# One streaming-encoder layer on one core: the program unrolled in groups of two tiles, without DRAM scratch, with a ring of seven slots and three buffers for the streamed weights

## The chip, the core and the metric

The kernel runs on one core of one Trainium2 chip. Its engines are TensorE (PE in the profile), VectorE (DVE), ScalarE (ACT), GpSimd (POOL) and SyncE (SP), each with its own instruction stream; they meet at semaphores. The metric is the device time of one execution in microseconds, as the median of several runs. All data is fp32.

## The reference

One layer over 1024 prompt frames and 32 sample frames of width 1024. Cut to what matters:

```
proj = rmsnorm(x) @ w_in                         # columns q|k|v|g (4 x 512), B|C|h (3 x 512)
q, k = rotary(q) * 128**-0.5, rotary(k)          # 4 heads of 128
o    = retention(state, q, k, v)                 # decayed scores @ v + decayed q @ state; state update
o    = rms_scale(o) * silu(g)
c    = B * short_conv(C * h)                     # 3 taps, 2 past rows
x    = x + concat[o, c] @ w_out
xn   = rmsnorm(x)
# PEER, per token and for each of 8 heads:
s1, s2 = keys1 . q1, keys2 . q2                  # 128 scores each
v1,i1 = top16(s1); v2,i2 = top16(s2)
top,sel = top16(v1[:,None] + v2[None,:])         # of 256 pairs
e    = i1[sel]*128 + i2[sel]; gate = softmax(top)
x    = x + sum_k gate_k * gelu(xn . u_tab[e_k]) * v_tab[e_k]      # 8 x 16 experts
y    = rmsnorm(x)
```

The state and the last two conv rows of both request groups are outputs too.

## The kernel before, in words

The tokens are nine tiles: eight of 128 prompt tokens and one of 32 sample tokens. For every token 128 expert rows (u and v side by side, 8 KB) are gathered from the table `uv`. One gather is an indirect DMA from GpSimd (line 445): one row for each of the 128 tokens of a tile, 1 MB, into one of `RING` = 8 slots of `ring`. Eight tiles of 128 gathers and one of 32 (the sample's tokens are spread over the partitions four times) make 1056.

What happens with gather k of a tile, in `experts` on each engine: VectorE multiplies the u half with `xn_cur` and sums it into `dots` (line 1033); ScalarE applies gelu (L585); VectorE multiplies with the gate (`weigh`, L1027), but only after the dot of gather k+1; ScalarE scales the v half (L581); TensorE adds it with eight transposing matmuls to `expert_sum` (L741) and raises `slot_free`, on which GpSimd waits before it gathers into the slot again.

Before all this, `projection` runs for all tokens, in two groups: GROUP_A (tile 0) and GROUP_C (the other seven prompt tiles and the sample). Its results go to DRAM, `proj_scratch` and `conv_scratch`. Between the gathers of tile t, the `mixer` of tile t+1 is woven in: a generator yields slot numbers (S_ROPE to S_PICK), `advance` runs its next piece when the loop has come to that slot, and each engine has the same slots, 64 per tile, one for two gathers. The mixer loads q, k, v, g from the scratch, does rotary, retention, W_out (L687), the second norm, the queries (L724; eight of the 16 weight blocks are resident, eight are streamed through two buffers `wq_buf`), the keys (L711), the top-16 search (L942 to L970) and the choice of indices and gates (L975 to L1006). The choice works on all eight heads of a tile at once, so that the index tile `idx_next` is complete only at its end; GpSimd copies it to `idx_cur` (L452) and then starts the next tile. The tiles 0 to 6 are a hardware loop (`Fori`) on each engine. At a tile's end ScalarE moves the sums out of PSUM (L596), TensorE transposes them back (L755) and the final norm writes y.

Each engine works in the order of its own program; a wait holds all that stands behind it. SP issues the loads in the same way.

Of the kernel before, what the change touches and what calls it, by code (L numbers as in the profile page):

```python
# [18 lines left out]
TILES = SEQ // P  # L35
H = 4
RET = H * P
CH = (D - RET) // P
PH = 8
# [5 lines left out]
SAMPLE_STEPS = STEPS // QUADS  # L45
RING = 8
PAIR = 2
SLOTS = STEPS // PAIR
WQ_RES = 8
WBUF = 2  # L50
STREAMED = BLK - WQ_RES
TOK_A = P
TOK_C = TOK - TOK_A
# [3 lines left out]
UNITS = CONV_UNITS + RET_UNITS  # L57
# [4 lines left out]
S_ROPE, S_KDECAY, S_QKT, S_SCORES, S_DECAYED, S_OUT, S_GATED, S_GATEDT = 2, 4, 5, 6, 7, 8, 9, 12  # L62
S_WOUT = 13
S_X1, S_XN, S_XNT = 21, 22, 23
S_QUERY = 25
S_TOP = 31
S_PAIRS = 47
S_BEST = 48
S_PICK = 56


class Group:
# [4 lines left out]

    def __init__(self, t0, tiles, buffers, earlier=None):
        self.t0, self.tiles, self.buffers = t0, tiles, buffers
        self.sample = tiles[-1] == DEC  # L80
        self.tok = sum(tiles)
        self.prompt = self.tok - (DEC if self.sample else 0)
        self.chunks = [(lo, min(lo + 512, self.tok)) for lo in range(0, self.tok, 512)]
        self.uses = [(3 * c + part, kind, i) for c in range(CH) for part, kind in enumerate("ChB")
                     for i in range(len(self.chunks))]
        self.conv_uses = len(self.uses)
        self.uses += [(CONV_UNITS + u, "tile", i) for u in range(RET_UNITS) for i in range(len(tiles))]
        self.by_act = [kind in ("tile", "C") for _, kind, _ in self.uses]

        self.block_ops = 5 + 4 * self.sample  # L90
        self.per = dict(uses=len(self.uses), act=sum(self.by_act), dve=len(self.uses) - sum(self.by_act),
                        ops=CH * self.block_ops, tiles=RET_UNITS * len(tiles), blocks=CH)
        self.before = {what: earlier.before[what] + earlier.per[what] if earlier else 0 for what in self.per}

        self.loads_before = [len(range(b, UNITS, earlier.buffers)) if earlier else 0 for b in range(buffers)]
        assert self.per["uses"] % 2 == 0 and self.conv_uses % 2 == 0

    def count(self, what, n=0):

        return self.before[what] + n  # L100

    def end(self, what):
        return self.count(what, self.per[what])

    def taken(self, q):

        who = "act" if self.by_act[q] else "dve"
        return who, sum(x == self.by_act[q] for x in self.by_act[:q + 1])

    def last_use(self, unit):  # L110
        return max(q for q, use in enumerate(self.uses) if use[0] == unit)

    def slot(self, q):

        return 1 + q * (SLOTS - 2) // len(self.uses)


GROUP_A = Group(0, [P], 4)
GROUP_C = Group(1, [P] * (TILES - 1) + [DEC], 2, GROUP_A)


def layer_kernel(nc, xT, x, w_ret, w_conv, w_out, wq, keysT, uv, g_mix, g_ffn, g_fin, conv_par,
                 ret_state, cos_sin, decay_p, decay_s, edge_p, edge_s, block_decay, ident, sel, iota,
                 y, out_ret_p, out_ret_s, out_conv_p, out_conv_s):
    proj = nc.dram_tensor("proj_scratch", (TOK, 4 * RET), F32).ap()
    convT = nc.dram_tensor("conv_scratch", (CH * P, TOK), F32).ap()

    with ExitStack() as ctx:
# [3 lines left out]
        def sem(name):  # L132
            return ctx.enter_context(nc.semaphore(name))


        ring = sb("ring", [P, RING, 2 * D])
        arena = sb("arena", [P, 7680])
# [3 lines left out]
        x1_next = sb("x1_next", [P, D])  # L141
        xn_next = sb("xn_next", [P, D])
        xn_cur = sb("xn_cur", [P, D])
# [3 lines left out]
        sel_sb = sb("sel_sb", [P, DEC])  # L147
# [6 lines left out]
        state = sb("state", [P, H, P])  # L154
        top_v = sb("top_v", [P, BLK, TOPK])
        top_i = sb("top_i", [P, BLK, TOPK], U32)
        idx_next = sb("idx_next", [P, STEPS], I32)
        idx_cur = sb("idx_cur", [P, STEPS], I32)
        gate_next = sb("gate_next", [P, PH, TOPK])
        gate_cur = sb("gate_cur", [P, STEPS])  # L160
        dots = sb("dots", [P, STEPS])
        weights = sb("weights", [P, STEPS])
        reduced = sb("reduced", [P, 2 * PH])
        stat = sb("stat", [P, 8])
# [3 lines left out]
        new_tail = sb("new_tail", [P, CH, 2, 2])  # L168


        flat = ring[:, :, :].rearrange("p r d -> p (r d)")
        xn_a = flat[:, 0:KC * TOK_A].rearrange("p (k t) -> p k t", k=KC)
        xn_c = flat[:, KC * TOK_A:KC * TOK].rearrange("p (k t) -> p k t", k=KC)
        at = KC * TOK
        units = [flat[:, at:at + KC * UNIT], flat[:, at + KC * UNIT:at + 2 * KC * UNIT],
                 arena[:, 0:KC * UNIT], arena[:, KC * UNIT:2 * KC * UNIT]]
        at += 2 * KC * UNIT
        rstd_all = flat[:, at:at + TOK]
        squares = flat[:, at + TOK:at + 3 * TOK].rearrange("p (b t) -> p b t", b=2)
        gate_c = flat[:, at:at + TOK_C]  # L180
        conv_y = flat[:, at + TOK_C:at + 2 * TOK_C + 2]
        conv_out = flat[:, at + 2 * TOK_C + 2:at + 3 * TOK_C + 2]
        taps = flat[:, at + 3 * TOK_C + 2:at + 4 * TOK_C + 6]
        assert at + 4 * TOK_C + 6 <= RING * 2 * D
        ones = xn_cur[:, 0:P]
        stored = xn_cur[:, P:P + 2 * UNIT].rearrange("p (b n) -> p b n", b=2)
        wq_buf = wq_sb[:, WQ_RES:]


        qkvg = arena[:, 0:2048]  # L190
        rot = arena[:, 2048:3072].rearrange("p (g c) -> p g c", g=2 * H)
        swap = arena[:, 3072:4096].rearrange("p (g c) -> p g c", g=2 * H)
        qkT = swap
        k_dec = arena[:, 4096:4608].rearrange("p (h c) -> p h c", h=H)
        decayed = arena[:, 4608:5120].rearrange("p (h c) -> p h c", h=H)
        ret_sq = decayed
        ret_o = arena[:, 5120:5632].rearrange("p (h c) -> p h c", h=H)
        catT = arena[:, 5632:6656].rearrange("p (k c) -> p k c", k=KC)
        xnT = catT
        qT = arena[:, 6656:7680].rearrange("p (g b c) -> p g b c", g=2, b=4)  # L200
        pairs = arena[:, 0:2048].rearrange("p (h i j) -> p h i j", h=PH, i=TOPK)
        scores = arena[:, 2048:4096].rearrange("p (b n) -> p b n", b=BLK)
        onehot = arena[:, 2048:4096].rearrange("p (k j) -> p k j", j=TOPK)
        left = arena[:, 5120:5376]
        best_v = arena[:, 5376:5504].rearrange("p (h k) -> p h k", h=PH)
        best_i = arena[:, 5504:5632].bitcast(U32).rearrange("p (h k) -> p h k", h=PH)
        half_i = arena[:, 5632:5888].bitcast(U32).rearrange("p (s k) -> p s k", s=2)
        half_f = arena[:, 5888:6144].rearrange("p (s k) -> p s k", s=2)
        pick_f = arena[:, 6144:6400].rearrange("p (s k) -> p s k", s=2)
        top_f = arena[:, 6400:6656].rearrange("p (b k) -> p b k", b=BLK)  # L210
        y_sb = arena[:, 6656:7680]
        sum_T = arena[:, 2048:3072].rearrange("p (k t) -> p k t", k=KC)
        folded_T = arena[:, 3072:3072 + KC * DEC].rearrange("p (k t) -> p k t", k=KC)


# [4 lines left out]
        bank = [expert_sum[:, 0:512], expert_sum[:, 512:D]]  # L220
        rms_ps = [x1_ps[:, 0:512], x1_ps[:, 512:D], tp[:, 1, 0:DEC]]


        consts_in = sem("consts_in")
        eps_set = sem("eps_set")
        xT_in = sem("xT_in")
        g_mix_in = sem("g_mix_in")
        unit_in = [sem(f"unit_in{i}") for i in range(GROUP_A.buffers)]
        squared = sem("squared")
        summed = sem("summed")  # L230
        rooted = sem("rooted")
        normed = sem("normed")
        projected = sem("projected")
        act_took = sem("act_took")
        dve_took = sem("dve_took")
        stored_out = [sem("stored_out0"), sem("stored_out1")]
        par_in = sem("par_in")
        conv_ops = sem("conv_ops")
        conv_out_done = sem("conv_out_done")
        tails_out = sem("tails_out")  # L240
        inits = sem("inits")

        tile_in = sem("tile_in")
        silu_done = sem("silu_done")
        rotated = sem("rotated")
        qkT_ready = sem("qkT_ready")
        qkT_copied = sem("qkT_copied")
        scores_ready = sem("scores_ready")
        decayed_ready = sem("decayed_ready")
        ret_ready = sem("ret_ready")  # L250
        ret_squared = sem("ret_squared")
        ret_rooted = sem("ret_rooted")
        gated = sem("gated")
        gatedT_ready = sem("gatedT_ready")
# [68 lines left out]
        def started(generator):  # L323
            return [generator, -1]
# [821 lines left out]
```

## Time and profile before

| | us |
|---|---|
| median of 3 runs (lowest, highest) | 3466.18 (3463.09, 3477.43) |
| the profiled execution | 3462.3 |
| its span, first to last instruction | 3459.0 |
| DVE busy | 2058.5 (60%) |
| PE busy | 2394.0 (69%), granted clock 0.824 on average |
| ACT busy | 1578.4 (46%) |
| DMA, mean over the span | 354 GB/s, 1225 MB |

The span is that of the profiled execution, the time is that of the whole execution around it. Busy shares are means over stages that differ much, so they are to be read by stage. A clock of 1.0 is 2.4 GHz for TensorE, 0.5 is 1.2 GHz, values between are means over a stretch.

### The profile page before, as it was taken

How to read it: one execution, taken by the hardware profiler on the slowest of the kernel's cores; microseconds unless marked ns; L12 is line 12 of the kernel's file. 1: busy time of each engine (PE TensorE's matmuls, PEld its weight loads, DVE VectorE, ACT ScalarE, POOL GpSimd, SP SyncE). 2: the span in 40 equal slices, each digit the busy share in tenths (PEclk: the TensorE clock that was granted, in tenths of full speed). 3: DMA queues.
4: the chain of work that ended last, by engine and by line, in shares of the span. 5: the costliest groups of instructions: out<-in, count | busy, mean ns of one | idle time of the engine just before them, and what ended most of it. 6: DMA issues, size and time to landing. Idle time of an engine off the chain costs nothing.

```text
span 3459.0 us, 43882 instructions
## 1 busy us (share of the span) xinstructions
PE 2394.0 (69%) x13716; PEld 1975.8 (57%) x13716; DVE 2058.5 (60%) x5356; ACT 1578.4 (46%) x2528; POOL 1256.1 (36%) x1076
## 2 busy tenths in 40 slices
PE   5799997676577657765776567647765676477756
PEld 4456885565457545754575457535754575346645
DVE  2121152568766876687668666866687667656774
ACT  1000113554555455445544554455545554455454
POOL 0000002444444544454344344434444444344434
PEclk8899997897789778976897799769977897778666
DMA  4612225999999999999999999989999999989987
GB/s 165 256 54 69 79 74 214 421 420 410 399 421 419 410 391 421 419 408 391 421 419 405 394 418 420 404 357 408 420 407 398 421 420 409 372 343 410 420 336 324
DMA packets 195395, 1225.07 MB, mean 354 GB/s; under 512 B 23568, under 2 KB 38864, under 8 KB 56592
## 3 DMA queue, kind: packets, MB, share of 16 engines
q0 software_dynamic: 152064, 1107.36, 78.0%
q1 hardware_dynamic: 32304, 103.66, 8.0%
q10 hardware_dynamic: 10752, 10.82, 0.9%
q8 instruction: 119, 1.95, 0.2%
q14 instruction: 156, 1.28, 0.1%
HBM read 1206.09 MB, written 15.67 MB: 353 GB/s over the span
## 4 chain that ended last, share of the span: by engine, by line
DMA 36%; PE 28%; issue 15%; DVE 13%; ACT 6%; SPq 1%; DVEq 0%; another core or an unknown queue 0%; POOL 0%; POOLq 0%; ACTq 0%; PEldq 0%
DMA ring<-in_uv,idx_cur 30%; PE expert_sum L741 8%; PE expert_sum L641 7%; PE expert_sum L647 5%; ACT ring L581 5%; PE mm L724 4%; DVE ring L1033 3%; DMA wq_sb<-in_wq 2%; DMA arena<-conv_scratch 2%; PE x_ps L687 1%; DVE arena L970 1%; DVE arena L988 1%; DVE arena L966 1%; DVE arena L968 1%; DVE arena L995 1%
## 5 line engine op out<-in xcount | busy, mean ns | idle before, releaser
L741 PE MATMUL expert_sum<-ident_sb,ring 128*128 128x128 f32 x8448 | 1421.6, 330 | 912.0 <-ACT ring L581 895.5
L741 PEld LDWEIGHTS expert_sum<-ident_sb,ring 128*128 128x128 f32 x8448 | 1207.9, 172 | 1139.0 <-ACT ring L581 1112.9
L445 POOL DMA_INDIRECT ring<-in_uv,idx_cur x1056 | 1245.1, 1179 | 1602.9 <-PE expert_sum L741 1339.7
L1033 DVE CUSTOM_DVE_ANT_0 ring<-ring,xn_cur 128x1024 f32<-128x1024 f32 x1056 | 1290.3, 1223 | 677.1 <-DMA ring<-in_uv,idx_cur 644.0
L581 ACT ACTIVATE ring<-ring,weights 128x1024 f32<-128x1024 f32 x1056 | 1196.3, 1134 | 0.0
L585 ACT ACTIVATE dots<-dots 128x1 f32<-128x1 f32 x1056 | 212.8, 201 | 1084.5 <-DVE dots L1033 1076.8
L724 PE MATMUL mm<-arena,wq_sb 128*128 128x128 f32 (+1 forms) x2304 | 311.6, 293 | 31.8 <-DMA wq_sb<-in_wq 31.8
L724 PEld LDWEIGHTS mm<-arena,wq_sb 128*128 128x128 f32 x2304 | 300.5, 210 | 36.8 <-DMA wq_sb<-in_wq 35.1
L641 PE MATMUL expert_sum<-ring 128*128 128x256 f32 (+1 forms) x1088 | 240.8, 380 | 1.9 <-DMA ring<-in_w_ret 1.1
L641 PEld LDWEIGHTS expert_sum<-ring 128*128 128x128 f32 (+1 forms) x1088 | 194.0, 181 | 43.5 <-issue 6.7
L452 POOL COPY idx_cur<-idx_next 128x64 int32<-128x64 int32 x16 | 10.8, 672 | 571.8 <-DVE idx_next L1006 571.8
L647 PE MATMUL expert_sum<-ring 128*128 128x512 f32 (+2 forms) x480 | 168.0, 511 | 42.4 <-DMA w_out_sb<-in_w_out 23.0
L1027 DVE TENSOR_TENSOR weights<-dots,gate_cur 128x1 f32<-128x1 f32 x1056 | 164.6, 156 | 25.4 <-ACT dots L585 23.4
L647 PEld LDWEIGHTS expert_sum<-ring 128*128 128x128 f32 x480 | 87.2, 200 | 120.1 <-issue 77.2
L497 ACT ACTIVATE xn_cur<-expert_sum 128x256 f32<-128x256 f32 x72 | 27.6, 383 | 279.6 <-PE expert_sum L641 262.3
L687 PE MATMUL x_ps<-w_out_sb,arena 128*128 128x512 f32 (+1 forms) x288 | 143.9, 624 | 0.0
L942 DVE MAX8 top_v<-arena 128x8 f32<-128x128 f32 (+1 forms) x144 | 41.1, 285 | 112.5 <-ACT arena L560 112.5
L1033 DVE DVE_READ_ACCUMULATOR2_ANT dots<- 128x1 f32 x1056 | 86.8, 82 | 0.0
L877 DVE TENSOR_TENSOR arena<-arena,cs_sb 128x1024 f32<-128x1024 f32 (+1 forms) x9 | 11.0, 1225 | 116.8 <-DMA arena<-conv_scratch 116.8
L555 ACT ACTIVATE arena<-mm 128x512 f32<-128x512 f32 (+1 forms) x36 | 20.2, 562 | 126.7 <-PE mm L724 108.4
L492 ACT ACTIVATE ring<-expert_sum 128x128 f32<-128x128 f32 (+2 forms) x12 | 5.6, 464 | 152.3 <-PE expert_sum L647 147.2
L687 PEld LDWEIGHTS x_ps<-w_out_sb,arena 128*128 128x128 f32 (+1 forms) x288 | 49.5, 190 | 42.2 <-issue 42.1
(129 smaller groups left out, 1317.2 us busy)
## 6 DMA issues: line engine op xcount, KB each, us to landing
wq_sb<-in_wq SPq DMA_DIRECT2D x80, 512.0 KB, 10.0
ring<-in_uv,idx_cur POOLq DMA_INDIRECT x1056
ring<-in_w_ret SPq DMA_DIRECT2D x12, 1024.0 KB, 5.1
ring<-in_w_conv SPq DMA_DIRECT2D x18, 512.0 KB, 3.9
proj_scratch<-xn_cur ACTq DMA_DIRECT2D x64, 128.0 KB, 1.9
arena<-proj_scratch SPq DMA_DIRECT2D x8, 1024.0 KB
arena<-in_w_ret SPq DMA_DIRECT2D x4, 1024.0 KB, 7.8
w_out_sb<-in_w_out SPq DMA_DIRECT2D x1, 4096.0 KB, 18.6
```

Of the source, the lines that this page charges most:

```text
L445: pool.indirect_dma_start(ring[:, k % RING, :], None, uv, bass.IndirectOffsetOnAxis(ap=idx_cur[:, k:k + 1], axis=0)).then_inc(landed[k % R ...
L581: act.activation(v, v, ACT.Copy, scale=weights[:, k:k + 1]).then_inc(scaled, 1)
L585: act.activation(dots[:, k:k + 1], dots[:, k:k + 1], ACT.Gelu_apprx_tanh).then_inc(gelu_done, 1)
L641: ins = pe.matmul(bank[q % 2][0:m, 0:UNIT], xn[:, k, i * P:i * P + m], w[:, k, :], start=(k == 0), stop=(k == KC - 1))
L647: ins = pe.matmul(bank[q % 2][:, 0:hi - lo], w[:, k, :], xn[:, k, lo:hi], start=(k == 0), stop=(k == KC - 1))
L687: ins = pe.matmul(x1_ps[0:n, j * 512:(j + 1) * 512], catT[:, k, 0:n], w_out_sb[:, k, j * 512:(j + 1) * 512], start=(k == 0), stop=(k == KC ...
L724: ins = pe.matmul(mm[:, g % 2, j * P:j * P + n], w_of(b)[:, k, :], xnT[:, k, 0:n], start=(k == 0), stop=(k == KC - 1))
L741: ins = pe.matmul(expert_sum[:, c * P:(c + 1) * P], ring[:, k % RING, D + c * P:D + (c + 1) * P], ident_sb[:, :], is_transpose=True, start ...
L942: op(dve.max(top_v[0:n, b, 0:8], s))
L966: op(dve.match_replace(rest, best_v[0:n, h, 0:8], s, LOWEST))
L1027: dve.tensor_tensor(weights[:, k:k + 1], dots[:, k:k + 1], gate_cur[:, k:k + 1], ALU.mult).then_inc(weighed, 1)
L1033: dve.tensor_tensor_reduce(u, u, xn_cur[:, :], 1.0, 0.0, ALU.mult, ALU.add, dots[:, k:k + 1]).then_inc(dotted, 1)
```

## The change

The two-stage program is replaced by one that is written out for all gathers, without a hardware loop. The tiles form four groups, (0, 1), (2, 3), (4, 5) and (6, 7, sample). A slot is now one gather; all work of group j is placed on slots from `base_of(j)` = 256 (j - 1) on, so group 0 lies at negative slots (its choices reach into the first 91 gathers), and group j+1 lies beside the gathers of group j. Within a group: norm at 6, 16 or 24 retention uses from 20 on (every 9 slots a unit), 12 conv uses from 92, mixers from 94 (18 slots each), W_out from 138 (12 each), then head by head queries and choices, 15 slots per head (21 in the last group, 13 in group 0).

- No DRAM scratch: q, k, v, g and the conv output stay in SBUF (`qkvg`, `conv_out`).
- All projection and query weights are streamed once per group, 22 blocks of 1 MB, through three buffers (`stream`); the resident query weights are gone.
- `RING` is 7.
- Queries and conv work on the 256 tokens (288 in the last group) of a group at once.
- Choices are made for one head of one tile at a time, with indices and gates in four rotating tiles (`idx`, `gate`); GpSimd waits once for every 16 gathers (`chosen`) and copies nothing. The one-hot work of a choice is on 512 columns instead of 2048, for one head.
- The exponentials are done in 26 batches (`GATES`) instead of nine.

The core of the diff:

```
-RING = 8
+RING = 7
+GROUPS = [(0, 1), (2, 3), (4, 5), (6, 7, SAMPLE)]
+RET_AT, RET_EVERY = 20, 9
+CONV_AT, CONV_EVERY = 92, 3.5
+MIX_AT, MIX_EVERY = 94, 18
+OUT_AT, OUT_EVERY = 138, 12
+def base_of(j):
+    return 2 * STEPS * (j - 1)
+def head_at(j, h):
+    if j == 0:
+        return 13 * h - 18
+    return turn_at(j, len(GROUPS[j])) + 2 + (15 if len(GROUPS[j]) == 2 else 21) * h
+def choose_at(j, h, i):
+    return head_at(j, h) + 5 + 7 * i
+def batches_of(t):
+    if t == 0:
+        return [(h, h) for h in range(PH)]
+    if t == 6:
+        return [(0, 1), (2, 3), (4, 5), (6, 7)]
+    return [(0, 3), (4, 7)]
-    proj = nc.dram_tensor("proj_scratch", (TOK, 4 * RET), F32).ap()
-    convT = nc.dram_tensor("conv_scratch", (CH * P, TOK), F32).ap()
-        wq_sb = sb("wq_sb", [P, WQ_RES + WBUF, KC, P])
+        stream = sb("stream", [P, 3, 2 * D])
+        idx = sb("idx", [P, 4, STEPS], I32)
+        gate = sb("gate", [P, 4, STEPS])
...
 def _(sp):
+                for i, (_, _, kind, j, n) in enumerate(STREAM):
+                    if i < 3:
+                        yield FIRST + 2
+                    else:
+                        slot, semaphore, count = used(i - 3)
+                        yield slot + 1
+                        sp.wait_ge(semaphore, count)
+                    dst = stream[:, i % 3, :]
...
 def _(pool):
-            with pool.Fori(0, TILES) as t:
-                wait_apart(pool, chosen, t + 1)
-                take(t, 0)
-                gathers(t * STEPS, range(0, 2 * RING))
-                take(t, 1)
-                gathers(t * STEPS, range(2 * RING, STEPS))
+            for g in range(TOTAL):
+                t, k = tile_of(g)
...
+                elif k % TOPK == 0:
+                    j = group_of(t)
+                    pool.wait_ge(chosen, pick(j, k // TOPK, t - GROUPS[j][0]) + 1)
+                if g >= RING:
+                    pool.wait_ge(slot_free, g - RING + 1)
...
 def _(pe):
-            with pe.Fori(0, TILES - 1) as t:
-                experts(t, STEPS, P, mixer(t + 1, P))
+            for g in range(TOTAL):
+                advance(programs, g)
+                t, k = tile_of(g)
...
+                pe.wait_ge(scaled, g + 1)
+                for c in range(KC):
+                    ins = pe.matmul(expert_sum[:, c * P:(c + 1) * P], ring[:, g % RING, D + c * P:D + (c + 1) * P],
...
 def _(dve):
+            def choices(j):
+                for h in range(PH):
+                    for i, t in enumerate(GROUPS[j]):
...
+                        for s in range(2):
+                            yield at + s
+                            if s == 0:
+                                dve.wait_ge(keyed_copied, c + 1)
+                            best16(tv[:, s, :], ti[:, s, :], scores[0:n, s, :], left[0:n, s * NK:(s + 1) * NK],
+                                   c + 1 if s else None)
+                        yield at + 2
...
+                        yield at + 3
+                        best16(bv, bi, pairs[0:n].rearrange("p i j -> p (i j)"), left[0:n])
+                        settle()
...
+            for g in range(TOTAL):
...
+                dve.wait_ge(landed[g % RING], 16 * (g // RING + 1))
+                u = ring[:, g % RING, 0:D]
+                dve.tensor_tensor_reduce(u, u, xn[:, t % 3, :], 1.0, 0.0, ALU.mult, ALU.add,
+                                         dots[:, g % RING:g % RING + 1]).then_inc(dotted, 1)
+                if g:
+                    weigh(g - 1)
+                advance(programs, g)
```

TensorE runs the pieces of slot g before the transposes of gather g, VectorE and ScalarE after the dot and the gelu of gather g.

## Rows read from the trace of the kernel before

**Rows 1.** The page's 40 slices of the span: GB/s moved by DMA.
```profile
GB/s 165 256 54 69 79 74 214 421 420 410 399 421 419 410 391 421 419 408 391 421 419 405 394 418 420 404 357 408 420 407 398 421 420 409 372 343 410 420 336 324
```
**Rows 2.** Windows: length, busy PE PEld DVE ACT POOL, PE clock, DMA share, GB/s.
```profile
0.00:562.50 562.50, 499.46 (x2153) 359.14 (x2154) 122.89 (x330) 60.63 (x127) 0.44 (x5) 0.96 0.31 110
562.50:3459.00 2896.50, 1894.56 (x11565) 1616.65 (x11563) 1935.63 (x5026) 1517.76 (x2401) 1255.63 (x1071) 0.80 0.98 402
```
**Rows 3.** DMA queues: packets, MB, share of 16 engines (gathers, then SP).
```profile
q0 software_dynamic: 152064, 1107.36, 78.0%
q1 hardware_dynamic: 32304, 103.66, 8.0%
```
**Rows 4.** The same windows view over the phases of one tile.
```profile
1267.00:1509.00 242.00, 170.36 (x1107) 147.66 (x1108) 156.19 (x427) 132.51 (x213) 109.72 (x92) 0.86 1.01 419
1509.00:1561.00 52.00, 30.34 (x155) 25.72 (x153) 45.06 (x128) 23.02 (x39) 25.47 (x20) 0.71 0.99 399
1561.00:1590.00 29.00, 16.52 (x85) 14.38 (x86) 28.49 (x48) 16.86 (x26) 12.67 (x10) 0.65 1.00 405
1590.00:1612.00 22.00, 11.18 (x69) 9.42 (x67) 6.63 (x16) 11.50 (x17) 8.80 (x9) 0.73 0.86 332
```
**Rows 5.** Timeline, one slot's life in a quiet phase: start, us, engine, line.
```profile
1357.18 1.23 DVE L1033 CUSTOM_DVE_ANT_0 ring<-ring,xn_cur 128x1024 f32<-128x1024 f32 x1 [1.18 <-DMA ring<-in_uv,idx_cur]
...
1361.03 1.13 ACT L581 ACTIVATE ring<-ring,weights 128x1024 f32<-128x1024 f32 x1
...
1362.39 1.04 PE L741 MATMUL expert_sum<-ident_sb,ring 128*128 128x128 f32 x8
...
1364.24 0.94 POOL L445 DMA_INDIRECT ring<-in_uv,idx_cur  x1 [1.65 <-PE expert_sum L741]
```
**Rows 6.** Timeline, the first gather's issue and the first dot.
```profile
562.50 1.10 POOL L445 DMA_INDIRECT ring<-in_uv,idx_cur  x1 [25.27 <-PEq L763]
...
569.46 1.23 DVE L1033 CUSTOM_DVE_ANT_0 ring<-ring,xn_cur 128x1024 f32<-128x1024 f32 x1 [32.39 <-DMA ring<-in_uv,idx_cur]
```
**Rows 7.** The prelude: one window of loads, then rows of its timeline.
```profile
10.00:15.00 5.00, 0.00 (x0) 0.00 (x0) 0.00 (x0) 0.00 (x0) 0.00 (x0) 1.00 1.06 403
...
16.46 0.31 ACT L473 ACTIVATE ring<-ring 128x128 f32<-128x128 f32 x1 [14.34 <-DMA ring<-in_xT]
...
37.73 6.75 DVE L779 RECIPROCAL ring<-ring 128x1056 f32<-128x1056 f32 x1 [36.05 <-ACT ring L478]
...
46.63 8.85 DVE L786 SCALAR_TENSOR_TENSOR ring<-ring,g_mix_sb 128x928 f32<-128x928 f32 x8
...
89.54 7.07 PE L641 MATMUL expert_sum<-arena,ring 128*128 128x256 f32 x32
```
**Rows 8.** Groups by line, engine and shape: busy us, mean ns; then idle before.
```profile
L687 PE MATMUL x_ps<-w_out_sb,arena 128*128 128x512 f32 x256 | 126.9, 620 | 0.0
...
L988 DVE TENSOR_TENSOR arena<-iota_sb,arena 128x2048 f32<-128x2048 f32 x16 | 36.6, 2285 | 0.1
...
L881 DVE TENSOR_TENSOR arena<-arena,cs_sb 128x512 f32<-128x512 f32 x8 | 5.5, 684 | 0.0
```
**Rows 9.** Timeline of VectorE: best-16 of 128, then a dot, best-16 of 256.
```profile
1488.15 0.29 DVE L942 MAX8 top_v<-arena 128x8 f32<-128x128 f32 x1
...
1490.07 1.21 DVE L1033 CUSTOM_DVE_ANT_0 ring<-ring,xn_cur 128x1024 f32<-128x1024 f32 x1
...
1523.11 1.22 DVE L1033 CUSTOM_DVE_ANT_0 ring<-ring,xn_cur 128x1024 f32<-128x1024 f32 x1
...
1524.34 0.42 DVE L963 MAX8 arena<-arena 128x8 f32<-128x256 f32 x1
...
1527.19 1.29 DVE L1033 CUSTOM_DVE_ANT_0 ring<-ring,xn_cur 128x1024 f32<-128x1024 f32 x1 [0.19 <-DVE arena L970]
```
**Rows 10.** Groups by line of ScalarE: the table loads around the exponentials.
```profile
L585 ACT ACT_TABLE_LOAD x41 | 52.6, 1283 | 0.7
...
L565 ACT ACT_TABLE_LOAD x9 | 11.5, 1283 | 0.5 <-ACT xn_cur L497 0.4
```

More of the change, by code:

```diff
@@ L35 @@
 TILES = SEQ // P
+SAMPLE = TILES
 H = 4
@@ L56 @@
 CONV_UNITS = 3 * CH
-UNITS = CONV_UNITS + RET_UNITS
 EPS = 1e-6
 LOWEST = -3.0e38
[L62 to L115, printed above, removed]
@@ new lines, in group_of, with width, column, place @@
+def group_of(t):
+    return min(t // 2, len(GROUPS) - 1)
+def base_of(j):
+    return 2 * STEPS * (j - 1)
+def width(j):
+    return sum(rows_of(t) for t in GROUPS[j])
+def column(t):
+    return P * (t - GROUPS[group_of(t)][0])
+def place(t):
+    return ORDERS[group_of(t)].index(t)
+def turn_at(j, r):
+    return base_of(j) + OUT_AT + OUT_EVERY * len(GROUPS[j]) + 2 * r
+def head_at(j, h):
+    if j == 0:
+        return 13 * h - 18
+    return turn_at(j, len(GROUPS[j])) + 2 + (15 if len(GROUPS[j]) == 2 else 21) * h
@@ new lines, with use_at, taken, taken_all @@
+USES_BEFORE = [sum(len(u) for u in USES[:j]) for j in range(len(GROUPS) + 1)]
+def use_at(j, kind, unit, t=None):
+    return [x[:3] for x in USES[j]].index((kind, unit, t))
+def taken(j, q):
+    flat = [x[0] for u in USES[:j] for x in u] + [x[0] for x in USES[j][:q + 1]]
+    by_act = flat[-1] in ("ret", "C")
+    return "act" if by_act else "dve", sum((k in ("ret", "C")) == by_act for k in flat)
+def taken_all(j):
+    flat = [x[0] for u in USES[:j + 1] for x in u]
+    by_act = sum(k in ("ret", "C") for k in flat)
+    return by_act, len(flat) - by_act
@@ new lines, in _ @@
+            programs = started(*[finish(t) for t in range(TILES + 1)],
+                               *[stage(j) for j in range(4) for stage in (norm, projection)],
+                               *[stage(t) for t in RANK for stage in (retention, out)],
+                               *[stage(j) for j in range(4) for stage in (queries, exponentials)], quads())
+            for slot in range(FIRST, 0):
+                advance(programs, slot)
+            for g in range(TOTAL):
+                act.wait_ge(dotted, g + 1)
+                d = dots[:, g % RING:g % RING + 1]
+                act.activation(d, d, ACT.Gelu_apprx_tanh).then_inc(gelu_done, 1)
+                if g:
+                    scale(g - 1)
+                advance(programs, g)
@@ L613, in _ @@
+            scale(TOTAL - 1)
+            for slot in range(TOTAL, LAST + 1):
+                advance(programs, slot)
         @block.tensor
         def _(pe):
[L616 to L622 removed]
@@ L756, in experts @@
                 ins.then_inc(sum_back, 1)
-            together(mixer(0, P), projection(GROUP_C))
-            pe.wait_ge(act_took, GROUP_C.end("act"))
-            pe.wait_ge(dve_took, GROUP_C.end("dve"))
-            pe.wait_ge(conv_out_done, 16 * GROUP_C.end("blocks"))
-            pe.sem_inc(slot_free, RING)
-            with pe.Fori(0, TILES - 1) as t:
-                experts(t, STEPS, P, mixer(t + 1, P))
-            experts(TILES - 1, STEPS, P, mixer(TILES, DEC))
-            experts(TILES, SAMPLE_STEPS, DEC)
+            programs = started(*[back(t) for t in range(TILES + 1)],
+                               *[stage(j) for j in range(4) for stage in (norm, projection)],
+                               *[stage(t) for t in RANK for stage in (retention, out)],
+                               *[queries(j) for j in range(4)])
@@ new lines, in gates @@
+            def gates(j):
+                for _, last, i, first in [b for b in GATES if b[0] == j]:
+                    t = GROUPS[j][i]
+                    n, heads = rows_of(t), last - first + 1
+                    yield choose_at(j, last, i) + 8
+                    b = GATES.index((j, last, i, first))
+                    dve.wait_ge(exp_done, b + 1)
+                    g = gate[0:n, t % 4, first * TOPK:(last + 1) * TOPK].rearrange("p (h k) -> p h k", k=TOPK)
+                    op(dve.tensor_reduce(reduced[0:n, 0, 0:heads], g, AX_X, ALU.add))
@@ new lines, in _ @@
+            programs = started(*[finish(t) for t in range(TILES + 1)],
+                               *[stage(j) for j in range(4) for stage in (norm, conv)],
+                               *[stage(t) for t in RANK for stage in (retention, out)],
+                               *[stage(j) for j in range(4) for stage in (choices, gates)], quads())
+            for slot in range(FIRST, 0):
+                advance(programs, slot)
+            for g in range(TOTAL):
+                t, k = tile_of(g)
+                if k == 0:
+                    if t == SAMPLE:
+                        dve.wait_ge(quads_xn, QUADS)
+                    else:
+                        dve.wait_ge(xn_ready, RANK[t] + 1)
+                dve.wait_ge(landed[g % RING], 16 * (g // RING + 1))
+                u = ring[:, g % RING, 0:D]
+                dve.tensor_tensor_reduce(u, u, xn[:, t % 3, :], 1.0, 0.0, ALU.mult, ALU.add,
+                                         dots[:, g % RING:g % RING + 1]).then_inc(dotted, 1)
+                if g:
+                    weigh(g - 1)
+                advance(programs, g)
@@ L1061 @@
+            weigh(TOTAL - 1)
+            for slot in range(TOTAL, LAST + 1):
+                advance(programs, slot)
 _OUTS = [("y", (TOK, D)), ("ret_p", (P, H, P)), ("ret_s", (P, H, P)), ("conv_p", (P, CH, 2)), ("conv_s", (P, CH, 2))]
```

1311 lines of the change are left out of this document (645 added, 666 removed).

## The prediction

> **What bounds the kernel now.** I read the page's slices first: under 260 GB/s in the first six, near 420 in most of the others [rows 1]. Two windows give the parts exactly: in the first 562.5 us the DMA engines are 0.31 busy and TensorE works 499 us; from the first gather on, DMA is 0.98 busy at 402 GB/s, TensorE 0.65, VectorE 0.67 and ScalarE 0.52 of the time [rows 2]. So there are two kernels in one: a prelude of 562.5 us that projects all 1056 tokens before any expert row is fetched, and a stage of 2896.5 us that is a stream of 1056 gathers. The queue rows say what streams: the gathers are 1107 MB, everything that SP moves is 104 MB [rows 3]. At 402 GB/s the second stage moved 1164 MB.
>
> Next I cut one tile of the second stage into its phases [rows 4]. In the 242 us where VectorE is 0.65 busy the DMA gives 419 GB/s, 2.50 us per gather of 1.049 MB. In the phases in which the top-16 lists are searched VectorE is 0.87 and then 0.98 busy and the rate falls to 399 and 405 GB/s. Around the tile's end (22 us) it is 332. So the stream is DMA-bound, with VectorE nearly level with it for a fifth of each tile, and a dip at each tile's end: there GpSimd waits until the new indices are complete, L452, and then a whole ring's length for the old tile's sums.
>
> Third, the life of a ring slot in a quiet phase [rows 5]: its dot starts at 1357.18, its weight is formed only behind the next dot, ScalarE scales at 1361.03, TensorE adds by 1363.43, GpSimd's next gather into it is issued by 1365.18. That is 8.0 us of processing. Eight slots at 2.50 us are 20.0 us, so 12.0 us are left for the gather itself, where the first gather of the empty stream landed 7.0 us after its issue began [rows 6].
>
> **The change, part by part.**
>
> *The prelude.* It now holds only tiles 0 and 1: norm, 16 retention uses, 12 conv uses, two mixers, one head's queries and one choice. Norm: xT arrives at about 9 us (1 MB of the 4.3 MB that had landed by 16.46 at about 400 GB/s [rows 7]); squares and sums took 20 us for 1056 columns, which I put at 8 for 256; the reciprocal is a quarter of 6.75, 1.7; eight scalings are about 3 where 928 columns took 8.85 [rows 7]; with table load and hops the projection starts at 25 us. A use of eight 256-column matmuls is 7.07/4 = 1.77 us [rows 7]: 16 are 28 us. Three 1 MB weight buffers are ahead of the constants on SP, but the fourth unit is queued behind some 9 MB of constants, w_out, keys and x, 23 us at 400 GB/s, so TensorE waits about 7 us for it: 60. Conv is 12 x 1.77 = 21 us of TensorE, woven with two mixers whose VectorE work is some twelve operations per tile on 512 columns (0.68 us [rows 8]) or 1024 (a dot is one: 1.23 [rows 5]), handed back and forth between three engines: I take 45 us, 105. W_out is 16 matmuls of 0.50 us per tile [rows 8], 8 us, twice, with norm and transposes behind each: 28, so 133. Queries, keys and the first choice: 3.5 + 3 + 10.3, so the first gather is issued at about 150 us. The bounds are 125 (conv hidden under the mixers) and 225 (all steps in series, the matmuls at half clock, as the granted clock falls to 0.71 and 0.65 in phases with little matmul work [rows 4]). Gain 410 us of 562.5.
>
> *What moves into the stream.* The other three groups' projections. Bytes: weights are now loaded once per group, 4 x 22 blocks of 1.049 MB; some 16 fall in the prelude, so 72 blocks, 75.5 MB, are in the stream, with x, xT, y, rotation tables and instructions about 90 MB; with the gathers 1197 MB against 1164. The scratch round trip goes. At 419 GB/s the stream costs 2857 us, at the whole-stage 402 it costs 2978.
>
> *Which rate?* Choices are the hungry phase. Per tile and head VectorE does two best-16 of 128 (1.92 us each when backlogged, 1488.15 to 1490.07), one of 256 (2.85, 1524.34 to 1527.19) [rows 9], a sum of 256 and two converts (0.7), small index operations with an equality over 512 (1.3, from 0.68 for 512 columns [rows 8]), and a product, a reduction and a convert (1.6): 10.3 us. Eight heads are 82 us per tile; the same sums for before are 31 + 23 + 18 = 72, because the one-hot work was in 2.29 us operations [rows 8] with fewer waits between. A dot with its weight costs 1.23 us when backlogged (1523.11 to 1524.34 [rows 9]). A group's choices lie in 120 slots: 16 x 10.3/120 + 1.23 = 2.6 us per gather, with gates and finishes 2.65; DMA there needs 2.50 plus 8 weight blocks over 120 slots, 2.67. Level, as in before, so I take the rate which before shows when they are level, 400 GB/s. Slots with choices are 91 + 120 + 120 + 168 = 499 of 1056; with 39 weight blocks (31 of queries, 8 of group 1's retention) they move 564 MB: 1410 us. The other 633 MB at 419: 1511. The next tile's indices are there long before they are needed and nothing copies them, so half of the 4.6 us which a tile's end loses now (22 us at 332) stays, mostly ScalarE's eviction of the sums: 8 x 2.3 = 18. End behind the last landing 10. Stream: 2949.
>
> *Costed at nothing, with the cover.* Conv, norm and mixers on VectorE: some 45 us in the 136 slots of a group without choices, where VectorE has 2.50 - 1.23 = 1.27 us spare in each; uncovered, 3 x 45 = 135. The projections on TensorE: 28 uses of 1.77 = 50 us per 256 gathers, 0.2 us per gather beside 1.0 of transposes [rows 5] and 0.2 of queries; at half clock twice that, 2.8, which would be over 2.50 and cost 0.3 x 256 x 3 = 230 us, but a busier TensorE had the higher clock in [rows 4] (0.86 against 0.71). Every step waits in order: behind a query on TensorE stand the transposes that free slots, behind ScalarE's copy the scale, behind VectorE's choice the dots. Each consumer step sits a slot or more after its producer, so a wait should be under one gather.
>
> *The ring of seven.* 17.5 - 8.0 = 9.5 us are left in flight, where 7.0 suffice [rows 5, 6]: cover for a stall falls from 5.0 to 2.5 us. Nothing, as long as steps stay near 3 us; a stall of 5 us in each choice would lose 2.5 us x 70 choices = 175.
>
> *Exponentials.* 26 batches in place of 9, each with a table load before it and Gelu's after it: 17 x 2 x 1.283 = 44 us of ScalarE [rows 10], which is busy 1518 us in the 2896 of the stream, 1.44 of 2.74 us per gather [rows 2]. Hidden: nothing; uncovered 44. The Trainium skill, ScalarE: Activation LUTs, section Table sets: the hidden batching unit, says to do all calls of one table set together, which speaks against this part. It gives about 2.66 us per switch with the drain, 90 us for these 34 by its figure. The trace agrees on 1.283 us for the load; no row shows a drain beside it.
>
> **The sum.** 150 + 2949 = 3099 us of span, and 3.3 that the profiled execution's 3462.3 has over its span 3459.0: 3102, say 3100. The median of the runs is 3.9 above that execution, which is nothing here.
>
> **The rivals.**
> 1. *Everything hides.* Prelude 125, stream 2857 at 419 GB/s, end 10: 2995. For it: the quiet phases hold 419 with extra work in them. Against: VectorE level with DMA in half the slots. Chance 0.10.
> 2. *The prelude is a chain.* 225 us, so 3175. For it: hand-offs with nothing behind them, and a cold clock. Chance 0.12.
> 3. *Choices stall the short ring.* Denser and more finely cut steps make VectorE need 3.0 to 3.2 us in choice slots, waits included, and the rate over the stream is 380: 3150, in all 3310 (3220 to 3400). For it: 2.5 us of cover, 14 waits in each choice. Against: such steps run at 400 GB/s now. Chance 0.14.
> 4. *The table loads show.* Each Exp holds ScalarE and with it the weights and dots: 44 us by [rows 10], 3145. Against: ScalarE's 1.3 us spare per gather. Chance 0.05. This is what the rule of the Trainium skill, ScalarE: Activation LUTs, Table sets: the hidden batching unit, warns of.
> 5. *Slower than before.* One mechanism: in-order waits between the four engines lengthen a slot's processing. The stream must exceed 3310 us, 3.13 per gather; seven slots then turn in 21.9 us, so processing would have to be 14.9 us, not 8.0, on average over all 1056. At 16 it is 7 + 16 = 23 us per seven, 3470 for the stream, 3620 in all. Against: 400 GB/s in the phases with the most inserted work. Chance 0.03.
> That the prelude stays as it was is excluded by the code: the first gather waits for the first head's choice, not for all projections.
>
> **How the numbers follow.** My forecast, 3100 with its own range 3040 to 3165, has 0.56. The range 3020 to 3250 takes in rivals 2 and 4 and the fringes of 1 and 3, and leaves about 0.2 out. About 0.5% (17 us) is what a measurement of this kernel can tell from no change. All cases but rival 5 are faster by far more; with 0.01 each for what I do not see: faster 0.95, within 0.5% 0.01, slower 0.04.
>
> **What would show it.** In the changed profile: first gather issued between 125 and 225 us; scratch queue gone and SP's queue near 115 MB; DMA share near 0.98 from there on, 415 or more in slots without choices, about 400 in them; VectorE near 0.95 busy in choices; no GpSimd wait of 16 us at a tile's end. The prediction is wrong if DMA share in choices falls under 0.9 with VectorE waiting on ScalarE or TensorE, or if the first gather comes after 225.

## The result and the profile after

The changed kernel takes 3338.41 us (median of 4 runs, 3338.12 to 3355.47) where the kernel before takes 3464.64 (4 runs, 3461.59 to 3477.43). The ratio is 0.9641, 95% interval 0.9602 to 0.968: faster by 3.6%, about a third of the gain that I forecast (3100), and outside the range of 3020 to 3250. The profiled execution is one of 3338.13 us, with a span of 3336.3.

The page of the changed kernel, its slices of GB/s and its two large queues, as in [rows 1] and [rows 3]:

```profile
GB/s 248 78 259 343 377 375 318 315 391 401 410 398 393 388 420 377 313 370 403 404 391 408 373 419 404 308 330 363 412 389 377 363 376 366 407 419 421 421 420 318
...
q0 software_dynamic: 152064, 1107.36, 82.9%
q1 hardware_dynamic: 31072, 113.80, 9.1%
```

The slow beginning is three slices now, but three new dips have come (318 315, 313, 308 330), 256 gathers apart. The windows view shows both, with the columns of [rows 2]: first the two parts, then stretches cut at the moments when GpSimd issues gathers 0, 96, 144, 256, 352, 400, 512 and 608 (the rows from 512.77, 1279.49 and 2047.59 are 48 gathers each), and the last 191 gathers:

```profile
0.00:198.46 198.46, 168.35 (x716) 131.88 (x716) 49.55 (x118) 32.70 (x61) 0.20 (x4) 0.95 0.40 144
198.46:3336.30 3137.84, 2270.14 (x11928) 1871.82 (x11928) 2094.17 (x6024) 1575.81 (x2565) 1172.07 (x1056) 0.80 0.96 381
...
198.46:512.77 314.31, 229.59 (x1236) 199.26 (x1236) 251.05 (x836) 151.77 (x255) 107.55 (x97) 0.84 0.93 367
512.77:691.04 178.27, 128.10 (x682) 113.75 (x683) 90.10 (x211) 83.71 (x128) 59.88 (x49) 0.81 0.87 327
691.04:1001.15 310.11, 227.11 (x1213) 184.64 (x1212) 235.78 (x723) 159.63 (x262) 120.82 (x113) 0.81 0.99 401
...
1279.49:1455.06 175.57, 127.63 (x682) 113.05 (x683) 90.21 (x209) 80.51 (x125) 57.68 (x49) 0.81 0.89 336
...
2047.59:2228.27 180.68, 135.45 (x697) 111.55 (x696) 93.64 (x225) 80.98 (x125) 53.55 (x49) 0.82 0.88 321
...
2545.32:2826.72 281.40, 193.19 (x968) 158.39 (x968) 240.44 (x790) 144.60 (x236) 109.85 (x96) 0.75 0.94 368
2826.72:3310.20 483.48, 329.41 (x1562) 269.18 (x1560) 260.51 (x623) 255.86 (x405) 192.05 (x192) 0.65 1.01 415
```

The first gather comes at 198.46, not at 150, and the stream behind it takes 3138 us, not 2949: 48 + 189 us too many. The stream's loss can be placed. The three rows of 48 gathers move 58.3, 59.0 and 58.0 MB (GB/s by us), which at the 419 that I took for slots without choices are 139, 141 and 138 us; they took 178, 176 and 181, 116 us more. These are the slots of the conv uses and of the mixers. The first 96 gathers, beside group 0's choices and group 1's first projections, are 26 us over what 400 GB/s would give, the 96 before the last row (the last group's choices) 23. That places 165 of the 189 us; the rest is not placed. The stalls in the choices of the middle groups that rival 3 feared are not there: 401 GB/s in 691 to 1001.

No engine is full in a conv stretch: TensorE is 128 of 178 us busy, VectorE 90. So it is waiting; the waits in 1279 to 1455 (engine, what waited for whom: us in all, times, longest):

```profile
POOL ring L474 <- PE expert_sum L813: 113.5, 43, 6.7
ACT dots L621 <- DVE dots L1094: 68.2, 22, 9.8
...
DVE conv_tmp L868 <- PE mm L675: 27.5, 4, 8.2
DVE conv_out L894 <- PE mm L675: 24.1, 4, 7.2
ACT conv_tmp L506 <- PE mm L675: 16.4, 4, 5.6
DVE ring L1094 <- DMA ring<-in_uv,idx: 13.6, 7, 3.6
```

The last row is the one that would be the longest of VectorE's waits in a DMA-bound stretch: VectorE waits only 13.6 us for landings and 51.6 for the banks of the conv uses. One such place in the timeline (start, us, engine, line):

```profile
1336.71 0.15 DVE L1076 TENSOR_TENSOR weights<-dots,gate 128x1 f32<-128x1 f32 x1
...
1336.94 1.13 ACT L610 ACTIVATE ring<-ring,weights 128x1024 f32<-128x1024 f32 x1
...
1338.12 1.97 PE L813 MATMUL expert_sum<-ident_sb,ring 128*128 128x128 f32 x8 [0.57 <-ACT ring L610]
...
1339.88 4.78 PE L675 MATMUL mm<-xn_in,stream 128*128 128x256 f32 x16
...
1344.50 1.04 PE L813 MATMUL expert_sum<-ident_sb,ring 128*128 128x128 f32 x8
1344.70 0.42 DVE L868 TENSOR_TENSOR conv_tmp<-mm,conv_tmp 128x256 f32<-128x256 f32 x1 [6.54 <-PE mm L675]
...
1348.31 1.22 DVE L1094 CUSTOM_DVE_ANT_0 ring<-ring,xn 128x1024 f32<-128x1024 f32 x1
1349.57 0.20 ACT L621 ACTIVATE dots<-dots 128x1 f32<-128x1 f32 x1 [7.34 <-DVE dots L1094]
```

VectorE comes to its conv step right behind its dots, at 1338.16, and finds that TensorE has not begun: the use stands in TensorE's order behind the transposes of the gather before (1338.12), which had to wait for that gather's weight (1336.71) and scale (1336.94), and then takes 4.78 us. VectorE stands 6.54 us, and by as much the next dot, at 1348.31, is late. ScalarE then stands 7.34 us for that dot, and behind its scale stand the transposes that free a slot.

And a use is longer than I took it. Groups of the page (as in [rows 8]), then pieces of the chain that ended last, in the prelude (start, us, what):

```profile
L669 PE MATMUL mm<-stream,xn_in 128*128 128x256 f32 (+1 forms) x1024 | 254.3, 405 | 6.2 <-DVE xn_in L848 6.2
L760 PE MATMUL mm<-turn,stream 128*128 128x256 f32 (+1 forms) x1024 | 255.0, 405 | 0.7 <-ACT turn L554 0.7
```

```profile
19.84 6.10 PE mm L669 x16
...
77.74 3.45 PE mm L675 x16
...
142.75 13.99 PE x_ps L729 x32
...
178.27 8.87 PE mm L760 x32
```

Each call of a matmul on f32 that does not transpose appears as two instructions: the queries are 8 heads of 16 calls in 4 groups, 512 calls, and the row has 1024. A use of eight calls is x16 and 3.45 us where the granted clock is 1.00 (25.94 to 77.74), W_out is x32 and 13.99 us per tile.

### The profile page after: what moved, and what is told of

Its sections match the earlier page's. It is cut to its first block, busy times and chain, and to the rows that moved or that the text cites. A ratio compares the mean times of both kernels' runs of the same rounds, so it can differ in the third digit from the quotient of the medians.

```text
span 3336.3 us, 36101 instructions
## 1 busy us (share of the span) xinstructions
PE 2438.5 (73%) x12644; PEld 2003.7 (60%) x12644; DVE 2143.7 (64%) x6141; ACT 1608.5 (48%) x2626; POOL 1172.3 (35%) x1060
## 3 DMA queue, kind: packets, MB, share of 16 engines
q1 hardware_dynamic: 31072, 113.80, 9.1%
## 4 chain that ended last, share of the span: by engine, by line
PE 39%; DVE 24%; DMA 18%; ACT 14%; issue 4%; POOL 1%; SPq 0%; DVEq 0%; POOLq 0%; ACTq 0%
DMA ring<-in_uv,idx 18%; PE expert_sum L813 14%; DVE ring L1094 10%; ACT ring L610 7%; PE mm L760 7%; PE mm L675 5%; PE mm L669 5%; PE x_ps L729 4%; ACT L621 1%; DVE pairs_left L977 1%; ACT dots L621 1%; DVE top_i L986 1%; DVE top_i L976 1%; PE tp L770 1%; DVE top_v L984 1%
## 5 line engine op out<-in xcount | busy, mean ns | idle before, releaser
L813 PE MATMUL expert_sum<-ident_sb,ring 128*128 128x128 f32 x8448 | 1495.3, 338 | 848.6 <-ACT ring L610 839.6
L474 POOL DMA_INDIRECT ring<-in_uv,idx x1056 | 1172.1, 1110 | 2138.6 <-PE expert_sum L813 1872.0
L813 PEld LDWEIGHTS expert_sum<-ident_sb,ring 128*128 128x128 f32 x8448 | 1241.1, 175 | 1110.0 <-ACT ring L610 1055.5
L1094 DVE CUSTOM_DVE_ANT_0 ring<-ring,xn 128x1024 f32<-128x1024 f32 x1056 | 1289.1, 1221 | 515.7 <-DMA ring<-in_uv,idx 508.3
L1076 DVE TENSOR_TENSOR weights<-dots,gate 128x1 f32<-128x1 f32 x1056 | 165.8, 157 | 146.7 <-ACT dots L621 146.7
L669 PE MATMUL mm<-stream,xn_in 128*128 128x256 f32 (+1 forms) x1024 | 254.3, 405 | 6.2 <-DVE xn_in L848 6.2
L760 PE MATMUL mm<-turn,stream 128*128 128x256 f32 (+1 forms) x1024 | 255.0, 405 | 0.7 <-ACT turn L554 0.7
L669 PEld LDWEIGHTS mm<-stream,xn_in 128*128 128x128 f32 (+1 forms) x1024 | 197.8, 198 | 46.8 <-DVE xn_in L848 6.6
L760 PEld LDWEIGHTS mm<-turn,stream 128*128 128x128 f32 x1024 | 203.5, 204 | 36.0 <-ACT turn L554 1.0
L675 PE MATMUL mm<-xn_in,stream 128*128 128x256 f32 (+1 forms) x672 | 181.1, 429 | 0.0
L675 PEld LDWEIGHTS mm<-xn_in,stream 128*128 128x128 f32 x672 | 143.8, 220 | 26.9
```

Source lines behind the costliest of these rows:

```text
L474: pool.indirect_dma_start(ring[:, g % RING, :], None, uv, bass.IndirectOffsetOnAxis(ap=rows, axis=0)).then_inc(landed[g % RING], 16)
L669: ins = pe.matmul(bank[0:n, 0:UNIT], xnj[:, k, at:at + n], weight[:, k, :], start=(k == 0), stop=(k == KC - 1))
L675: ins = pe.matmul(bank[:, 0:w], item[:, unit % 2, k, :], xnj[:, k, :], start=(k == 0), stop=(k == KC - 1))
L760: ins = pe.matmul(query_bank(j, s), weight[:, s, k, :], xnT_of_group(j)[:, k, :], start=(k == 0), stop=(k == KC - 1))
L813: ins = pe.matmul(expert_sum[:, c * P:(c + 1) * P], ring[:, g % RING, D + c * P:D + (c + 1) * P], ident_sb[:, :], is_transpose=True, start ...
L1076: dve.tensor_tensor(weights[:, at:at + 1], dots[:, at:at + 1], gate[:, 1 if t == SAMPLE else t % 4, k:k + 1], ALU.mult).then_inc(weighed, 1)
```

## The experiments

Theory A: the loss comes from the order of waits, a long use in TensorE's queue and a consumer one slot behind it. Theory B, the rival: the ring of seven is too short, and any irregularity shows. Theory C, which the expectations name too: these slots are simply full of work. Each edit is against the changed kernel. All but the last were run once each beside a run of the kernel before (3468.42 for the first four, 3462.68 for the others); e9 has four runs. Four runs of the changed kernel differ by up to 17 us, so a few us between single runs say nothing. Us between the issues of gathers (in the changed kernel, conv is 96 to 144, 352 to 400, 608 to 656; 400 to 512, 512 to 608 and 656 to 768 are left out):

```
                  after  e1    e2    e3    e5    e4    e6    e8    e7
time              3338   3262  3259  3300  3153  3467  3376  3203  3162
first gather       198    195   196   199   148   199   199   188   189
0-96               314    312   312   310   286   324   315   290   286
96-144 conv        178    147   147   173   156   178   178   151   143
144-256            310    314   311   306   302   332   320   304   304
256-352            278    278   276   278   279   296   279   287   278
352-400 conv       176    151   150   163   156   177   172   150   143
608-656 conv       181    159   160   180   160   190   182   159   154
768-864            281    281   282   280   267   290   284   265   264
864-1055           483    483   482   480   487   505   484   485   479
```

**e1_conv_lag: the conv consumers three slots behind the use.**

```
-                    yield slot + 1
+                    yield slot + (3 if kind == "C" else 1)
...
-                    yield USES[j][qh][3] + 1
+                    yield USES[j][qh][3] + 3
...
-                    yield USES[j][qb][3] + 1
+                    yield USES[j][qb][3] + 3
```

> The three consumers of a conv use (ScalarE's copy of C, VectorE's two products) run three slots behind TensorE's use instead of one; the work is the same. Theory A (VectorE and ScalarE stand in line for a use that TensorE starts more than a slot late and that takes 3.45 us or more): the slots 96 to 144 of groups 1 to 3 fall from 3.8 to about 2.9 us per gather, 3170 to 3220 us in all. Theory B (seven slots are too few to cover steps of this size) and theory C (these slots are simply full of work): no change, 3320 to 3350 us.

Measured 3262.12 us. The three conv stretches give 535 - 457 = 78 us of the 116, and the others stay within some 4 us: no byte, no operation and no buffer was changed, only places in the order. That shows A for these stretches, and excludes C for those 78 us. The gain is well short of the 118 us or more that I expected of A; 38 us of the loss stay in these stretches.

**e2_all_lag: the same for the retention uses too** (`yield slot + 3` for every projection consumer on ScalarE).

> As the run with the conv consumers three slots behind, and ScalarE's copies of the retention uses three slots behind as well. Theory A: the 56 waits of 3.2 us on ScalarE in slots 20 to 92 go too, a part of which was hidden: 20 to 60 us below the conv run, 3120 to 3190 us. Theories B and C: 3320 to 3350 us.

Measured 3258.7 us, 3 less than e1, where I expected 20 to 60: missed. The waits behind the retention uses were hidden. In the middle conv stretch the DMA is now nearly full, and of VectorE's waits there the one for landings is the longest, while those for conv banks are gone (windows of e2, then its waits):

```profile
1282.00:1427.00 145.00, 110.82 (x642) 91.71 (x641) 87.61 (x199) 79.77 (x123) 55.31 (x48) 0.89 0.97 389
```

```profile
DVE ring L1094 <- DMA ring<-in_uv,idx: 31.0, 21, 2.8
DVE turn L935 <- PE tp L707: 11.4, 2, 5.7
```

The first 96 gathers have not moved. In e2's waits there the same pattern stands at other names, the query's copy and the weights behind the gelu:

```profile
ACT qT L564 <- PE mm L760: 50.4, 6, 10.7
DVE weights L1076 <- ACT dots L621: 32.9, 11, 6.6
```

**e3_ring8: eight slots again, two weight buffers for three.**

```
-RING = 7
+RING = 8
...
-        stream = sb("stream", [P, 3, 2 * D])
+        stream = sb("stream", [P, 2, 2 * D])
```

> Eight ring slots, paid for by two stream buffers instead of three; all else as in the changed kernel. Theory B: the slots 96 to 144 gain most of what they lost, 3190 to 3240 us. Theory A: VectorE itself is held, so a longer ring helps only at the edges of the stretch, 3300 to 3338 us. If two stream buffers are too few, it is slower than 3345 us.

Measured 3300.17 us, 38 less, but only some 18 of it in the conv stretches (4.8, 12.8, 0.2): the dip stays. A longer ring softens what the waits do; it is not their cause. This kernel takes a weight buffer away as well, and what that costs alone was not tried.

**e5_half: half of the matmuls over k in projections, queries and W_out left out.** One of the four places:

```
-                        for k in range(KC):
+                        for k in (0, 1, 2, KC - 1):
```

> Leaves out half of the matmuls over k in the projections, the queries and W_out, so that a use costs what the prediction charged for it (some 1.75 us); all waits and slots stay. Theory A: 65 us less in the prelude, and each of the 36 conv waits in the stream shorter by 1.7 us, likewise queries and retention uses: 3130 to 3200 us. If TensorE's price is not what holds the stream, only the prelude gains: 3265 to 3285 us.

Measured 3152.79 us. The first gather comes at 148.31, where I had forecast 150 with uses at half their length, and the part behind it loses 135 us, 64 of them in the conv stretches and 29 in the first 96 gathers. Half-length uses are what I had costed, and the prelude agrees at each mark within 6 us, among them: conv and mixers end at 109.26 (I said 105), W_out with norms at 131.87 (133). Even the wait for the fourth weight unit is there, 10.87 us where I said 7; in the changed kernel the longer uses hide it (from the chain that ended last in e5):

```profile
26.51 10.87 DMA stream<-in_w_ret
...
109.26 7.12 PE x_ps L729 x16
...
131.87 5.12 PE mm L760 x16
```

**e4_ring6: six slots** (`RING = 6`).

> Six ring slots instead of seven, all else as in the changed kernel. If the ring's length sets the stream's pace (theory B), a slot less costs well over 100 us: 3440 us or more. If it only covers stalls that other engines make, as eight slots gave 38 us, it costs 30 to 80 us: 3370 to 3420 us.

Measured 3467.38 us, 129 more: all of the change's gain, and the outcome that I had put down to B. The conv stretches hardly move (178, 177, 190); choices and quiet stretches do. In a quiet one the changed kernel moves 421 GB/s and e4 403 (windows of after, then of e4):

```profile
3020.00:3180.00 160.00, 112.45 (x508) 89.70 (x506) 83.37 (x192) 79.31 (x128) 62.63 (x64) 0.62 1.01 421
```

```profile
3150.00:3300.00 150.00, 102.45 (x462) 82.17 (x463) 75.78 (x174) 71.20 (x116) 56.96 (x58) 0.61 1.00 403
```

By [rows 5, 6] six slots of 2.50 us less 8.0 of processing leave 7.0 in flight, just the 7.0 that the first gather took in an empty stream: no cover, by this estimate. So B is right about the ring's length in general, one slot below the one chosen, and wrong about the place of the loss.

**e6_exp72: one exponential batch for each head of each tile, 72 for 26.**

```
-    if t == 0:
+    if t < SAMPLE + 1:
         return [(h, h) for h in range(PH)]
```

> 72 batches of exponentials instead of 26, one per head and tile: 46 more batches, each with two table loads of 1.283 us on ScalarE (118 us) and three small operations on VectorE (some 0.8 us, 37 us). If the table loads were hidden, as forecast: up to 40 us slower, 3338 to 3378 us. If they show: 3420 to 3500 us.

Measured 3376.18 us, 38 more. The table loads of ScalarE by line, first in the changed kernel, then in e6:

```profile
L621 ACT ACT_TABLE_LOAD x57 | 73.1, 1283 | 1.0
L583 ACT ACT_TABLE_LOAD x26 | 33.4, 1283 | 0.5
```

```profile
L621 ACT ACT_TABLE_LOAD x103 | 132.1, 1283 | 1.8
L583 ACT ACT_TABLE_LOAD x72 | 92.4, 1283 | 1.3
```

Ninety-two more loads are 118 us of ScalarE, and at most 38 of them show. VectorE is 21 us busier in e6 (2164.8 for 2143.7, smaller operations in more batches; I had put 37), so what the loads alone cost is left open; it is at most a third of their length.

**e8_lag2: e2, and the query's copy, the choice and the second half of a retention step later too.**

```
-    return head_at(j, h) + 5 + 7 * i
+    return head_at(j, h) + 7 + 7 * i
...
-                    yield head_at(j, h) + 2
+                    yield head_at(j, h) + 4
...
-                yield at + 14
+                yield at + 15
```

> As the run in which all consumers of the projections run three slots behind (3258.7 us), and now also ScalarE's copy of the queries four slots behind the first query use instead of two, with the choices two slots later, and the second half of the retention steps one slot later. Theory A: ScalarE's six waits of some 8 us for the queries in slots 0 to 96 and VectorE's waits of 5.7 us for the retention matmuls go: 3190 to 3225 us. If these slots are full of VectorE's choices and nothing else: 3250 to 3260 us.

Measured 3203.2 us, 56 less than e2: 22 in the first 96 gathers, 17 in the last group's choices, 8 in the prelude, 5 to 9 in each of the other stretches of choices; one stretch (256 to 352) is 10 slower. The wait for the query's copy, 50.4 us in e2's first 96 gathers, is nearly gone (waits of e8, 188 to 478):

```profile
ACT qT L564 <- PE mm L760: 4.1, 3, 2.1
```

Which of the three moves gave what was not separated.

**e7_lag2_ring8: e8 with e3's ring of eight and two weight buffers.**

> The same later consumers with eight ring slots and two stream buffers. If cover for a stall is still what the short ring lacks, 25 to 45 us below the run with seven slots; if the later consumers leave no stalls, within 10 us of it.

Measured 3161.6 us, 42 less than e8. Its stream runs at 403 GB/s, near the rates that I forecast (windows, the two parts and two conv stretches):

```profile
0.00:195.00 195.00, 166.13 (x716) 130.41 (x716) 55.27 (x146) 33.95 (x62) 5.02 (x9) 0.95 0.43 154
195.00:3159.00 2964.00, 2202.17 (x11928) 1821.50 (x11928) 2088.41 (x5995) 1575.64 (x2563) 1169.82 (x1051) 0.81 0.99 403
...
474.94:617.65 142.71, 111.70 (x672) 97.80 (x672) 89.88 (x209) 80.62 (x124) 57.26 (x49) 0.90 0.97 384
...
1199.30:1341.95 142.65, 112.00 (x680) 98.25 (x680) 89.14 (x205) 79.30 (x124) 57.75 (x48) 0.90 0.98 399
```

**e9_best_timed: the kernel of e7, timed.**

> The version with later consumers, eight ring slots and two stream buffers again, timed in rounds beside the kernel before: 3155 to 3170 us, a ratio near 0.912.

3159.82 us (median of 4 runs, 3155.98 to 3164.1) beside 3466.71 (7 runs) of the kernel before: ratio 0.9095, interval 0.9051 to 0.9139. It beats both kernels; the change as made left 179 us on the table.

## Why the prediction was wrong

**The step that failed first is a size: "A use of eight 256-column matmuls is 7.07/4 = 1.77 us [rows 7]".** I took 32 instructions for four uses. They are two, because each call is two instructions, so a use is 3.45 us; with it fall "W_out is 16 matmuls of 0.50 us per tile" (32, 13.99 us) and the 3.5 us of a head's queries (8.87). The trace of before had told it twice. [Rows 8] have x256 for W_out over eight tiles, 32 per tile where the code calls 16. And ScalarE's copies in the old prelude, one behind each use, come 3.76 and 3.36 us apart:

```profile
93.20 0.38 ACT L497 ACTIVATE xn_cur<-expert_sum 128x256 f32<-128x256 f32 x1 [3.07 <-PE expert_sum L641]
...
96.96 0.38 ACT L497 ACTIVATE xn_cur<-expert_sum 128x256 f32<-128x256 f32 x1 [3.38 <-DMA proj_scratch<-xn_cur]
...
100.32 0.38 ACT L497 ACTIVATE xn_cur<-expert_sum 128x256 f32<-128x256 f32 x1 [2.98 <-DMA proj_scratch<-xn_cur]
```

**The prelude, 198 for 150.** By my own marks: the projection starts at 19.84 (I said 25), retention ends at 77.74 (60), conv and mixers at 142.75 (105), W_out with norms at 178.27 (133), the first gather is at 198.46 (150). So -5, +23, +20, +8, +3; in the second term the longer uses cost 30, and the 7 us that I had added for the fourth weight unit did not come. TensorE is 168 of the 198 us busy, so rival 2, a chain of hand-offs on a cold clock, was half right in its time and wrong in its cause: it is mostly work, at a granted clock of 0.95. e5, with half the work, lands at 148.

**The stream, 3138 for 2949: "Each consumer step sits a slot or more after its producer, so a wait should be under one gather."** A slot in the order is not a lead in time. From the timeline above: TensorE's use of a slot starts only when the transposes of the gather before are done, so from the weight that these need (1336.71) a scale, 1.97 us of transposes and 4.78 of the use must pass before VectorE's step at 1344.70, 8.0 us in all, while VectorE itself is at that step at 1338.16. With uses at half their length the waits are still 4.6 us on average (36.8/8), more than a gather, as e5's waits in the same stretch, 1170.67 to 1326.39, show:

```profile
DVE conv_tmp L868 <- PE mm L675: 18.8, 4, 5.4
DVE conv_out L894 <- PE mm L675: 18.0, 4, 5.1
```

There the conv stretches, at 471 us, keep some 53 of the 116 that they lose: this step was wrong by itself, and the first one made it worse. Shown by e1 and e8 (moving steps in the order alone takes 135 us out of the time) and by e5 (shortening the producers takes 186, 50 of them in the prelude). With both the lag and the eighth slot the stretch from first to last gather is 2943 us and the part behind the first gather 2971, where I forecast 2949: the rates of 400 and 419 were about right, and what was wrong was to take it that nothing stood in their way.

**The ring: "Nothing, as long as steps stay near 3 us".** The condition was the right one and it was not met: VectorE's waits for conv banks are 51.6/8 = 6.5 us on average, up to 8.2. The 2.5 us of cover that I worked out fits e4, where one slot less brings the quiet rate to 403. With the steps mended, the eighth slot is still worth 42 us, with a weight buffer given up for it.

**Rival 3**, choices stalling the short ring (3310, 3220 to 3400), came nearest in time and had the wrong place: choices in the middle groups ran at 401 and 396 GB/s, as costed. Its mechanism, finely cut steps in order with little cover, is the true one, but in the conv stretches and in the first and last choices. That the whole stream ran at 381 GB/s, where it has 380, is luck. Rival 5 stayed far off, rival 1 was excluded by the prelude alone.

**What came as written, and what did not.** SP's queue moves 113.80 MB (115 forecast), the scratch queue is gone; quiet slots run at 415 and more; the largest gap between two gathers at a tile's end is 5.1 to 7.4 us, where before most were 14 to 18. The rate in group 1's choices (gathers 168 to 288) is 402 GB/s, but not for the reason that I gave:

```profile
760.24:1102.95 342.71, 245.24 (x1354) 209.88 (x1352) 282.44 (x901) 174.06 (x292) 131.00 (x120) 0.81 1.00 402
```

VectorE is 0.82 busy there, not the 0.95 that I forecast, so it is not level with the DMA; what holds the rate is not shown. My sign of being wrong, a DMA share under 0.9 with VectorE waiting for TensorE, came in the conv stretches (0.87 to 0.89) and not in the choices where I had put it. The 26 exponentials are nearly hidden: 92 more loads cost no more than 38 us, so the 33 that their two lines gained (x57 and x26 for the x41 and x9 of [rows 10]) cost at most 14 by the same price, and are not what is missing. The Trainium skill, ScalarE: Activation LUTs, section What ACT_TABLE_LOAD costs, puts the load at about 1.283 us and a switch at 2.66 with the drain. The runs agree on 1.283 for the load; at 1338.09 the changed kernel's load of L532 begins as ScalarE's scale before it ends and its operation starts at 1339.38, so no drain of its size stands beside it here.

## What to carry to other kernels

Count the instructions of a trace row against the calls in the code before dividing its time by anything: x32 is four uses or two, and taking it for four was one of the two errors here. When work is woven into a stream by slots, put a consumer as many slots behind its producer as the producer's queueing and length last in time, not one; here one or two more slots on three engines were worth 135 us, with no operation, byte or buffer added. Size a ring by flight plus processing plus the longest stall, and when the stalls are mended ask again whether memory is better spent on a slot than on a weight buffer.

## What the runs showed of the hardware that I had not expected

A matmul call on f32 of 128x128 by 256 columns is two instructions of about 0.216 us each (3.45/16, in a stretch whose granted clock is 1.00); the transposing calls are one each (8448 = 1056 x 8 of L813). The DMA share does not tell the rate: it is 1.00 at 403 GB/s with six slots and 1.01 at 421 with seven. And much turns on one slot of the ring: six, seven and eight give 3467, 3338 and 3300 us, the last with a weight buffer less.
